# A hybrid attention and DeltaNet layer on one core: the last quarter of its MLP input product as seven block products

## The reference

```python
    for l in range(DEPTH):                     # DEPTH = 1
        h = rms_norm(x, pre_norm_mix[l])
        y = hybrid_mixer(h, w_in[l], ...)
        x = x + rms_norm(y, post_norm_mix[l])
        h = rms_norm(x, pre_norm_mlp[l])
        y = jnp.square(jax.nn.relu(h @ w_mlp_in[l])) @ w_mlp_out[l]
        x = x + rms_norm(y, post_norm_mlp[l])
```

## Time and profile before

| | |
|---|---|
| median of 3 executions | 749.78 us (749.64 to 750.03) |
| the profiled execution's own time | 749.47 us |
| its span, first to last instruction | 747.9 us |
| mean granted TensorE clock | 0.998 of full speed |
| busy in the span: PE, PEld | 99%, 81% |
| busy in the span: DVE, ACT, POOL | 59%, 52%, 43% |
| MLP input, first to last matmul | about 412 to 589 us |
| MLP output | 589 to 742 us |

### The profile page before, as it was taken

One profiled execution on the slowest core, in us unless ns is written; L12 is line 12 of the kernel. 1 busy time (PEld: TensorE's weight loads), 2 busy tenths in 40 slices (PEclk: granted clock), 3 DMA queues, 4 the chain that ended last, 5 costly groups with the idle time before them and its releaser, 6 DMA issues.

```text
span 747.9 us, 11901 instructions
## 1 busy us (share of the span) xinstructions
PE 739.4 (99%) x4168; PEld 607.1 (81%) x4168; DVE 438.7 (59%) x651; ACT 389.4 (52%) x632; POOL 318.5 (43%) x296
## 2 busy tenths in 40 slices
PE   9999999999999999999999999999999999999996
PEld 7788778888887878888878988888888888888885
DVE  5897899981444645345983512221221777778795
ACT  6657842268555364635645733333332655555671
POOL 2357894535444654564536464645645000000002
PEclk9999999999999999999999999999999999999999
DMA  9336124456366577266551279779887575654652
GB/s 340 104 95 202 57 81 104 127 128 186 117 158 155 196 163 208 69 150 214 206 170 28 85 241 293 191 259 286 194 275 204 153 234 196 195 189 151 216 177 113
DMA packets 52893, 129.21 MB, mean 173 GB/s; under 512 B 6096, under 2 KB 6512, under 8 KB 50544
## 3 DMA queue, kind: packets, MB, share of 16 engines
q1 hardware_dynamic: 49120, 109.47, 44.3%
q0 software_dynamic: 3392, 18.88, 13.1%
q10 hardware_dynamic: 336, 0.28, 0.1%
HBM read 126.49 MB, written 39.86 MB: 222 GB/s over the span
## 4 chain that ended last, share of the span: by engine, by line
PE 88%; DVE 4%; POOL 3%; ACT 2%; issue 1%; DMA 1%; SPq 0%; DVEq 0%; POOLq 0%; ACTq 0%
PE bank L758 27%; PE bank L759 26%; PE bank L760 26%; POOL rsq L2158 2%; PE bank L1005 1%; PE bank L1028 1%; PE bank L1015 1%; POOL w_lo L2164 1%; DVE bank L1884 1%; PE bank L969 1%; PE bank L933 1%; PE bank L788 1%; PE bank L980 1%; DMA raw<-in_w_out 0%; DVE w_lo L1638 0%
## 5 line engine op out<-in xcount | busy, mean ns | idle before, releaser
L2164 POOL TENSOR_TENSOR w_lo<-raw,w_hi 128x512 fp32r<-128x512 f32 x169 | 219.9, 1310 | 240.0 <-ACT w_hi L1220 238.2
L1220 ACT ACTIVATE w_hi<-raw 128x512 fp32r<-128x512 f32 (+2 forms) x214 | 145.1, 685 | 154.5 <-PE bank L760 118.7
L758 PE MATMUL bank<-h_hi,w_hi 128*128 128x512 f32 (+1 forms) x528 | 208.5, 395 | 0.2
L759 PE MATMUL bank<-h_lo,w_hi 128*128 128x512 f32 (+1 forms) x528 | 204.2, 387 | 0.0
L760 PE MATMUL bank<-h_hi,w_lo 128*128 128x512 f32 (+1 forms) x528 | 204.1, 386 | 0.0
L758 PEld LDWEIGHTS bank<-h_hi,w_hi 128*128 128x128 f32 x528 | 99.2, 188 | 25.8 <-issue 5.1
L760 PEld LDWEIGHTS bank<-h_hi,w_lo 128*128 128x128 f32 x528 | 99.2, 188 | 20.6
L759 PEld LDWEIGHTS bank<-h_lo,w_hi 128*128 128x128 f32 x528 | 99.3, 188 | 18.5
L1629 DVE SCALAR_TENSOR_TENSOR relu_sb<-bank,rs_row 128x512 f32<-128x512 f32 x32 | 20.6, 686 | 125.9 <-PE bank L760 114.2
L2302 POOL TENSOR_SCALAR ssh<-ssy 128x1 f32<-128x1 f32 x4 | 1.0, 238 | 151.6 <-ACT junk L1600 151.6
L758 PE MATMUL bank<-w_hi,a_hi 128*128 128x512 f32 x120 | 46.8, 390 | 0.0
(11 more groups left out here) (327 smaller groups left out, 1262.7 us busy)
## 6 DMA issues: line engine op xcount, KB each, us to landing
raw<-in_w_in SPq DMA_DIRECT2D x87, 256.0 KB, 2.7
raw<-in_w_mlp_in SPq DMA_DIRECT2D x62, 256.0 KB, 4.8
t_sum<-in_w_mlp_out POOLq DMA_DIRECT2D x12, 1024.0 KB, 9.4
raw<-in_w_mlp_out SPq DMA_DIRECT2D x26, 256.0 KB, 2.7
raw<-t_sum SPq DMA_DIRECT2D x26, 256.0 KB, 2.9
v_sum<-in_w_mlp_out POOLq DMA_DIRECT2D x4, 1024.0 KB, 9.4
raw_b<-in_w_mlp_out SPq DMA_DIRECT2D x16, 256.0 KB, 2.9
raw_b<-t_sum SPq DMA_DIRECT2D x14, 256.0 KB, 2.9
```

The lines of the kernel that those rows point to most:

```text
L758: pe.matmul(o, s_hi, m_hi, start=start, stop=False, skip_group_check=True)
L759: pe.matmul(o, s_hi, m_lo, start=False, stop=False, skip_group_check=True)
L1220: return a.activation(o, i_, ACT.Copy, scale=scale)
L2164: g.tensor_tensor(w_lo[:, slot, :], raw[:, slot, :], w_hi[:, slot, :].bitcast(F32), ALU.subtract).then_inc(lo_ready, 1)
```

## The change

The last quarter of the hidden features (groups 12 to 15, units 168 to 183 of before) is computed in the seven-product form too. Tokens are halved (256 each), inputs are halved (512 each), hidden features are halved (512 each). A step takes two blocks of 128 hidden features of each half through seven products; there are two steps. Each product takes two units, so a step has 14 units and the quarter 28 instead of 16, and every matmul has 256 columns instead of 512. U_M1 goes from 184 to 196.

- **Sums of weights:** four more sums of 1 MB (`u_copy`, `u_add`) in HBM, issued at units 48 to 68; the other ten of that stretch are placed anew. Of the 16 older sums the last two move: (3, 2) is copied in group 11 and added in the first step, (3, 3) is copied and added in the second.
- **Sums of tokens:** in groups 4 to 7 DVE adds h_hi and h_lo again (`full_block`), makes four sums (`t_blocks_made`) and their low halves (`t_low`), 12 operations of 128x1024; ACT rounds them (`ts_hi`). They lie where `x_res` and `pn_mlp` were, so SP copies x_res to HBM (four transfers of 512 KB, in groups 2 and 3), and POOL fetches it and pn_mlp back during the output phase (`late_in`).
- **Rings:** the loads of the quarter have eight slots instead of four; 10 of 14 low halves are made by DVE, 4 by POOL.
- **Post-additions:** per step ACT copies p1 (two of 128x256) and DVE makes e1, f, c11, c22, c12, c21 (two of 128x256 each) and `relu_in` (two of 128x768, over three blocks at once).
- **Row of scales:** ACT copies a second piece of it (`rs_ext`, 256 columns) before the first relu may start.

```diff
+SUM_AT = {64: (0, 0), 73: (1, 0), 76: (2, 0), 79: (0, 1), 82: (1, 1), 88: (2, 1)}
+IN_SUM_AT = {48: (0, 0), 51: (1, 0), 58: (2, 0), 68: (3, 0)}
+OUT_SUM_AT = {55: 0, 61: 1, 70: 2, 85: 3}
+IN_PRODUCTS = ("q1", "q6", "q5", "q2", "q7", "q3", "q4")
+LOW_POOL = (1, 3, 7, 11)
 # SP
+                    sp_.dma_start(x2_copy[t], x_res[:, t, :]).then_inc(copied_out, 16)
...
+        for s in range(STEPS_IN):
+            for v in range(PER_STEP):
+                u = U_S + PER_STEP * s + v
+                if v >= RING - RAW or s:
+                    sp_.wait_ge(*low_of(u - RING))
+                sp_.dma_start(raw_of(u), in_source(s, v)).then_inc(raw_signal(u)[0], 16)
+                if (s, v) == (1, 0):
+                    sp_.wait_ge(*added(3, 3))
+                    sp_.dma_start(*t_copy(3, 3)).then_inc(t_copied[3], 16)
 # PE
-        with pe.Fori(1, 8) as i:
+        with pe.Fori(1, G_PLAIN // 2) as i:
             mlp_in(i, False)
+            for half in range(2):
+                u = U_S + PER_STEP * s + 2 * IN_PRODUCTS.index(name) + half
+                pe.wait_ge(*low_of(u))
+                for kk in range(2):
+                    for e in range(2):
+                        c = slice(kk * 256 + e * P, kk * 256 + e * P + P)
+                        x_ = three(bank[IN_BANK[name] + e][:, 0:256], w_hi[:, u % SPL, c], w_lo[:, u % SPL, c],
+                                   *in_operand(name, 2 * half + kk), ...)
 # ACT, after the last unit
         a_split(1, 1, slice(0, 4))
-        square_group(NI - 1, 1)
         w_split(6, 2, 16)
+        for e in range(2):
+            square_in(STEPS_IN - 1, e)
 # DVE, after the last unit
-        relu(NI - 1, ms=(2, 3))
+        w_low(2, 1, 3)
+        v.wait_ge(unit_done, U_M1)
+        for e in range(2):
+            c21(STEPS_IN - 1, e)
         w_low(3, 1, 4)
         w_low(4, 2, 6)
         a_low(1, 1, slice(0, 4), 2)
+        for e in range(2):
+            relu_in(STEPS_IN - 1, e)
         w_low(6, 2, 8)
         s4(0)
 # POOL
+                if (s, v) == (0, 1):
+                    add_sum(3, 2)
+                if (s, v) == (1, 7):
+                    add_sum(3, 3)
+        for t in range(NT):
+            g.wait_ge(part_done, 24 + 8 * t)
+            g.dma_start(x_res[:, t, :], x2_copy[t]).then_inc(late_in, 16)
```

More of the change, by code:

```diff
@@ L187, in loads, with made @@
     return u // 4 + 1 - (1 if u >= U_X and u % 4 >= 2 else 0)
+def made(name, s, e):
+    return 14 * s + 2 * ("e1", "f", "c11", "c22", "c12", "c21", "relu").index(name) + e + 1
 STEPS = side_steps()
@@ L1494, in mlp_in @@
                     a.wait_ge(row_full, 1)
-                    mark(copy(rs_row[:], bank[7][:]), row_ready)
+                    mark(copy(rs_row, bank[7][:]), row_ready)
+                    mark(copy(rs_ext[:, 0:256], bank[7][:, 256:512]), row_ready)
                     square_group(i, 0)
[L1497 to L1502, removed]
+                if not (first and j < 3):
@@ new lines, in split_in, with mlp_in_last @@
+        def split_in(u):
+            a.wait_ge(*raw_signal(u))
+            a.wait_ge(unit_done, u - 3)
+            copy(w_hi[:, u % 4, :], raw_of(u)).then_inc(hi_ready, 1)
+        def mlp_in_last(i):
+            for j in range(8):
+                u = U_OUT + LEAD + 8 * i + j
+                if u < U_S:
+                    split(None, u % 4, 16 * loads(u), u - 3)
+                else:
+                    split_in(u)
+                if j in (3, 7):
+                    square_group(i, j // 4)
@@ new lines, in square_in, with mlp_in_step @@
+        def square_in(s, e):
+            a.wait_ge(made_in, made("relu", s, e))
+            for m in range(2):
+                a.activation(act_pair(G_PLAIN + 2 * s + e, slice(4, 6) if m else slice(0, 3, 2)),
+                             relu_sb[:, 2 * e + m, :].rearrange("p (s c) -> p s c", s=2), ACT.Square).then_inc(act_ready, 1)
+        def mlp_in_step(s):
+            for v in range(PER_STEP):
+                u = U_S + PER_STEP * s + v
+                if u + LEAD < U_M1:
+                    split_in(u + LEAD)
+                else:
+                    a.wait_ge(unit_done, u)
+                    w_split(u + LEAD - U_M1, 1, 16)
+                if v == 2:
+                    if s:
+                        a.wait_ge(made_in, made("c21", s - 1, 1))
+                    for e in range(2):
+                        copy(p1[:, e, :], bank[e][:, 0:256]).then_inc(p1_copied, 1)
+                if s and v in (3, 4):
+                    square_in(s - 1, v - 3)
+                if s == STEPS_IN - 1 and v == 8:
+                    a_split(0, 0, slice(0, 4))
@@ L2038, in _ @@
+        relu(0, True)
+        relu(1, ms=(0, 1))
+        combine(0)
+        relu(1, ms=(2, 3))
+        combine(1)
+        relu(2, ms=(0, 1))
+        combine(2)
+        for b in range(4):
+            full_block(b)
+        relu(2, ms=(2, 3))
+        combine(3)
+        t_blocks_made()
+        relu(3, ms=(0, 1))
+        combine(4)
+        for i in range(4):
+            t_low(i)
+        relu(3, ms=(2, 3))
+        combine(5)
+        for i in range(4, G_PLAIN // 2):
             relu(i, ms=(0, 1))
-            combine(i * 2 - 2)
+            combine(2 * i - 2)
+            if i == G_PLAIN // 2 - 1:
+                for u in range(U_S, U_S + LEAD):
+                    in_low(u)
@@ L2040, in _ @@
             relu(i, ms=(2, 3))
-            combine(i * 2 - 1)
-        relu(NI - 1, ms=(0, 1))
-        combine(2 * NI - 4)
-        combine(2 * NI - 3)
-        a_low(0, 0, slice(0, 4), 1)
-        for s in range(3):
-            w_low(s, 1, s + 1)
-        relu(NI - 1, ms=(2, 3))
+            combine(2 * i - 1)
+        for s in range(STEPS_IN):
+            step_in(s)
+        w_low(2, 1, 3)
+        v.wait_ge(unit_done, U_M1)
+        for e in range(2):
+            c21(STEPS_IN - 1, e)
         w_low(3, 1, 4)
```

301 lines of the change are left out of this document (252 added, 49 removed).

## The result

| | before | after |
|---|---|---|
| median of 21 executions each | 749.94 us (748.93 to 751.33) | 751.97 us (749.73 to 754.33) |
| ratio, 95% interval | | 1.0028 (1.0021 to 1.0036) |
| the profiled execution's own time | 749.47 us | 753.84 us |
| its span | 747.9 us | 752.1 us |

The change makes the kernel slower by 0.28%, about 2 us; 748.4 had been forecast. The profiled execution lies 1.9 us above the median of its kernel, so the losses found in it are of a bad but common execution (6 of the 21 lie above 753).

What follows compares the result with a forecast made beforehand. PE's own work was taken to bound the kernel (739.4 of 747.9 us busy). Terms -3.2 on PE and +1.8 at the exit, others 0, gave -1.4: median 749.78 to 748.4 us, range 746.8 to 751.2.

Steps and rivals of the forecast that it cites:

- The sum on PE: MLP input's last quarter: 43.5 us of matmuls removed, 40.3 added at 0.120 each; PE gains 3.2 us.
- The spacing that the Trainium skill gives for streams of weight loads: Quarter's matmuls: an estimated 98 ns for 256 columns, so 32.9 us for 25.2, a loss of 7.7 us; not adopted.
- the rival built on the weight loads: Quarter: 336 weight loads one after another take 49.1 us, 5.6 more than now; 757 us, chance 0.01.
- The exit: Start of output phase's i = 1: PE waits for a_low(2) behind relu_in and squares, on at 12.7 us, cost 1.8.
- the forecast's lower bound of 1.5: PE's wait at i = 1 of the output phase if relu_in costs the price of 512 columns: 1.5 us.
- Transfers in the quarter: Loads issued 9.5 us ahead with 2.1 to spare barely cover the longest landing of 11.1 us; cost 0.
- the bound of 11.6: Quarter's loads: a landing over 11.6 us (9.5 + 2.1) after its slot came free is too late.
- The rival: Late loads in the quarter, from SP's wait for an add and the (3, 3) copy: 752.6 (751.3 to 754), chance 0.15.
- the row of scales: Before the first relus of the MLP input: the second copy of 256 columns costs 0, at most 0.1 us.
- the entry: Start of the quarter: relus, squares, split and POOL's low half just fit ahead of its unit 3; cost 0 to 0.1.
- the copies of x_res: Groups 2 and 3: the four copies on the SP queue cost loads only time the ring has; cost 0.
- four more sums in units 48 to 88: Units 48 to 88: four more adds, each issue holding POOL 1.15 us; cost 0, upper bound 4.6 us.

Runs made afterwards that it cites:

- e9: e2 with one of the last relus behind each half of i = 1 on DVE, and ACT's squares half an i later than in e5; 747.11 us, ratio 0.9972.
- e2: Changed kernel with parts 6 and 7 loaded ahead of parts 0 and 1 of i = 1, SP's wait for the MLP input's end left out; 749.17 us, 0.9996.
- e10: e9 with parts 6 and 7 loaded late again, behind parts 0 and 1 of i = 1, as in the changed kernel; 748.96 us, ratio 0.9996.
- e1: Changed kernel with relu_in and the last four squares moved as a block behind a_low(2); 752.69 us, ratio 1.0037.
- e4: Changed kernel with the sums (3, 2) and (3, 3) moved out of group 11 and the quarter into the output phase; 751.97 us, ratio 1.0043.
- e7: e6 without the four copies of x_res to HBM (input x fetched back instead); 754.29 us, ratio 1.0054.
- e3: e1 and e2 together: relu_in and squares late, parts 6 and 7 early; 748.78 us, ratio 0.9992.
- e5: e2 with the block spread: one of the last relus and its squares behind each half of i = 1; 748.89 us, ratio 0.9994.
- e8: Changed kernel with only the relus and squares spread as in e5, parts 6 and 7 still late; 751.49 us, ratio 1.0038.
- e11: e9 without the four copies of x_res to HBM (input x fetched back instead); 747.55 us, ratio 0.9968.
- e12: e9 with the sums of the plain groups closed up by one, group 6 taking one, (3, 3) added at the quarter's first step; 748.73 us, ratio 0.9988.
- e6: e5 with sums (3, 2) and (3, 3) in the output phase and the fetches of x_res put off to its second half; 754.66 us, ratio 1.0069.

## Why the prediction was wrong

- **The sum on PE was right.** 40.31 us in e9, and in eight other of the 13 profiled executions of the changed quarter, for 40.3. So half the columns cost 53%, in place as in the sample. The spacing that the Trainium skill gives for streams of weight loads ("TensorE: Matmul & The Clock Gate", section "Back-to-back issue gap"), and the rival built on the weight loads, fell: 0.120 us each, with a load for every matmul, where the forecast estimated 0.098 from the page.
- **The exit was the step that failed, by its size.** Its place, its releaser and its chain (relu, squares, split, w_low, a_low) were as written, and paid once. But the working took the split of parts 6 and 7 as done when its turn came. In the kernel before, it stood behind the squares, and its load had landed 0.1 us earlier (589.77 + 3.0, for a split at 592.88); the change puts it ahead of the squares, and no term asked when its load lands. It landed 5.9 us into the phase instead of 3.6: SP reached its issue 0.5 us later, held up by low halves that DVE makes later, and the landing took 4.8 us instead of 3.0. This put the squares at 6.94 us instead of 5.33, and the exit at 3.25 instead of 1.8. e2 takes that out and measures 1.47, the forecast's lower bound of 1.5; e10 measures the late parts alone, against e9. How much of it is SP's order and how much the slower landing, no run separates.
- **The clock was in no term.** After the wait of 2.69 us the clock was at its lower level for eight matmuls: 1.69 us more. The waits of 2.25 in e1 and 2.50 in e4 were followed by it as well, that of 2.97 in e7 was not, nor were that of 1.55 in the quarter and those of 0.5 to 1.3 in e2, e3, e5, e8 and e10. What separates e7 from the others isn't settled. That the loss was common is likely from the mean granted clock: of the 21 executions of the changed kernel the 16 of 751.6 us and more have 0.997 or less, and four of the five under 751 have 0.998 or 0.999; in e9 all eleven have 0.998 or 0.999, and the 30 of the kernel before that ran beside e9 have 0.997 to 0.999.
- **Transfers in the quarter at 0: wrong in some executions.** The landing of 11.1 us that the term rested on was too short, and the bound of 11.6 too strict. PE waited in the quarter in three of the 13 profiled executions, those whose slowest group of loads from 520 to 546 us landed in 17.0 (the changed kernel), 15.3 (e2) and 16.0 us (e11); that cost 1.8, 1.1 and 1.0 us. In the others this group took at most 14.2 (e12, where the quarter took 40.46 us), and 13.8 in e9, where it cost nothing. The rival had the right engine and the wrong place: SP issued the copy of (3, 3) at 556.77, after the wait at 553.53, so no wait of SP for an add caused it. The rival's 751.3 to 754 holds the measured 751.97 by luck: what it priced is not what took the time. That the adds and loads of the quarter's entry share the DMA engines (share 1.03 from 547 to 554 us) is the likely cause: e4 takes the sums away, the loads land sooner and the wait is gone, though six profiled executions with the sums in place had none either (e1, e3, e5, e8, e9, e10). No new place tried for the sums was a gain (e4 as slow as the changed kernel, e6 slower than e5, e12 no faster than e9). How often an execution has this wait can't be read from medians.
- **Nothing, as forecast:** the row of scales (0.09 us), the entry (no wait), the copies of x_res (e11). For the four more sums in units 48 to 88: no wait of PE in that stretch is new, and in e9 the first product of w_out's last piece starts at 410.61, 0.2 us behind the one traced execution of the kernel before.
- **The net.** -3.2 + 1.8 was to be -1.4. The profiled execution has -3.2 + 1.8 (quarter) + 3.25 (exit) + 1.69 (clock) + 0.7 (late up to 411 us). The chance of "slower" stood on late loads almost alone; the exit, whose queue was worked out to 0.1 us, had no case above 2.1.

In e9 the median is 2.7 us under that of before and the ratio, which takes all executions, 2.1: some of its executions (748 to 749.2) still lose 1 to 2 us. That these are late loads is likely from e11's profiled execution (749.26), which had a wait of 1.26 us in the last plain group and one of 0.78 in the quarter, and not shown.

## What to carry to other kernels

When an edit adds an operation to one in-order queue and its consumer to another, place the consumer late enough to find its input made: the relu took 0.95 us of DVE, and up to 2.9 us of standing in ACT's queue when its consumer came first (e5). Follow each input of the chain back to the queue that issues its load and ask what that queue is waiting for ahead of it; here two loads whose slots the quarter no longer read stood 9 us behind a wait that was not theirs, and then passed one that only the kernel before had needed. A wait on the bounding engine can cost more than its length, so a forecast that puts one there needs a case in which the clock falls after it.

## What the hardware showed that was not expected

- The clock fell to half for 8 matmuls after a single wait of 2.3 to 2.7 us in a kernel that is otherwise at full clock (three profiled executions), and did not after one of 2.97 us (e7).
- Changes of place for 1 MB sums (and, in e6, for the fetches of x_res) move the time by up to 0.7% with the bytes unchanged: beside two adds and a copy the loads of the output phase shown under e6 landed in 6.5 us instead of 2.6, and five of six executions of e6 took 4 to 7 us more than the median of e5.
